# Normalising the two heads of an attention unit together, and copying the compressed probabilities one step earlier, in a two-layer hybrid transformer kernel

## The reference, cut to what matters

```python
o_a = banded_attention(qa, ka, heads(a_v, A_KV_HEADS), A_WINDOW, a_sinks)      # 4 heads, with sinks
o_b = causal_attention(jnp.concatenate([q_nope, q_pe], axis=-1), k_b, v_b)     # 4 heads
o_cmp, o_slc = nsa_compressed_selected(qc, qc_rot, k_cmp, v_cmp, k_slc, ...)   # 8 heads
o_win = banded_attention(qc_rot, k_win, heads(c_vw, C_KV_HEADS), C_WINDOW)     # 8 heads
gates = jax.nn.sigmoid(jax.nn.silu(c_gf) @ c_gate_w + c_gate_b).reshape(b, t, C_HEADS, 3)
o_c = gates[..., 0:1] * o_cmp + gates[..., 1:2] * o_slc + gates[..., 2:3] * o_win
o = jnp.concatenate([o_a.reshape(b, t, -1), o_b.reshape(b, t, -1), o_c.reshape(b, t, -1)], axis=-1)
return o @ w_out
```

## Time and profile before

| what | number |
|---|---|
| time, median of three runs | 1130.08 us (1129.71 to 1130.69) |
| the profiled execution's own time | 1130.08 us |
| its span, first to last instruction | 1128.3 us |
| PE busy | 1084.1 us, 96% of the span |
| DVE busy | 831.3 us, 74% |
| ACT busy | 499.5 us, 44% |
| the chain that ended last | PE 84%, DVE 11%, ACT 2% of the span |
| mean granted clock of PE | 0.989 of full speed |

### The profile page before, as it was taken

How to read it: one execution, slowest core, us unless ns; L and a number is a source line. 1 busy time by engine, 2 the same in 40 slices (tenths; PEclk the granted TensorE clock), 3 DMA queues, 4 the chain that set the end, 5 groups by cost and what they waited for, 6 DMA issues and landing times.

```text
span 1128.3 us, 13797 instructions
## 1 busy us (share of the span) xinstructions
PE 1084.1 (96%) x5221; PEld 837.4 (74%) x5221; DVE 831.3 (74%) x1502; ACT 499.5 (44%) x868; POOL 12.0 (1%) x30
## 2 busy tenths in 40 slices
PE   5999999999989999999999999999998999999998
PEld 1688888865766588888878888886576667888887
DVE  1766997886988785876687789886879787655644
ACT  2543342324567563343534433422255566433431
POOL 4000000000000000000000000000000000000000
PEclk9999999999989999999999999999998999999999
DMA  9799999454612179896439999954582113876631
GB/s 360 259 378 363 372 378 326 148 180 129 224 62 76 38 252 330 305 325 209 162 113 334 342 387 384 355 194 156 115 294 80 53 61 115 269 250 230 199 112 74
DMA packets 149366, 253.70 MB, mean 225 GB/s; under 512 B 9639, under 2 KB 119861, under 8 KB 141109
## 3 DMA queue, kind: packets, MB, share of 16 engines
q1 hardware_dynamic: 148596, 251.53, 65.1%
q10 hardware_dynamic: 704, 1.30, 0.3%
HBM read 251.76 MB, written 1.05 MB: 224 GB/s over the span
## 4 chain that ended last, share of the span: by engine, by line
PE 84%; DVE 11%; ACT 2%; issue 1%; DMA 1%; SPq 0%; DVEq 0%; ACTq 0%
PE ps L693 12%; PE ps L695 12%; PE ps L694 12%; PE ps L723 8%; PE ps L727 8%; PE ps L725 8%; PE ps L845 6%; DVE mwl L1915 2%; PE ps L705 2%; PE ps L674 1%; PE ps L672 1%; PE ps L673 1%; PE ps L901 1%; DMA wide<-in_ada_w_dram 1%; PE ps L890 1%
## 5 line engine op out<-in xcount | busy, mean ns | idle before, releaser
L693 PE MATMUL ps<-wh,uh 128*128 128x512 f32 x576 | 227.2, 395 | 0.0
L695 PE MATMUL ps<-wlo,uh 128*128 128x512 f32 x576 | 224.5, 390 | 0.0
L694 PE MATMUL ps<-wh,ul 128*128 128x512 f32 x576 | 224.3, 389 | 0.0
L1645 DVE TENSOR_TENSOR wlo<-wide,wh 128x1024 fp32r<-128x1024 f32 x176 | 207.6, 1220 | 15.7 <-ACT wh L1183 13.9
L1183 ACT CAST wh<-wide 128x1024 fp32r<-128x1024 f32 x176 | 175.9, 1049 | 16.7 <-DMA wide<-in_ffn_w_in_dram 16.7
L1255 ACT ACTIVATE fs<-ps 128x512 f32<-128x512 f32 x40 | 24.0, 599 | 282.3 <-PE ps L695 273.1
L1800 DVE TENSOR_TENSOR fa<-fs,ps 128x512 f32<-128x512 f32 x40 | 27.5, 688 | 137.8 <-ACT fs L1255 137.2
L723 PE MATMUL ps<-th,fh 128*128 128x512 f32 x320 | 128.1, 400 | 0.0
L695 PEld LDWEIGHTS ps<-wlo,uh 128*128 128x128 f32 x576 | 108.1, 188 | 23.0
L727 PE MATMUL ps<-tlo,fh 128*128 128x512 f32 x320 | 125.0, 390 | 0.0
L725 PE MATMUL ps<-th,fl 128*128 128x512 f32 x320 | 124.6, 390 | 0.0
(11 more groups left out here) (363 smaller groups left out, 1548.2 us busy)
## 6 DMA issues: line engine op xcount, KB each, us to landing
wide<-in_ffn_w_in_dram SPq DMA_DIRECT2D x176, 512.0 KB, 6.6
ada<-in_ada_w_dram SPq DMA_DIRECT2D x60, 1024.0 KB, 7.1
tall<-in_ffn_w_out_dram SPq DMA_DIRECT2D x44, 1024.0 KB, 5.2
wide<-in_w_in_dram SPq DMA_DIRECT2D x14, 1024.0 KB, 7.5
tall<-in_w_out_dram SPq DMA_DIRECT2D x8, 1024.0 KB, 8.6
ada<-in_ada_w_dram SPq DMA_DIRECT2D x16, 512.0 KB, 5.9
wide<-in_c_cmp_w_dram SPq DMA_DIRECT2D x4, 1024.0 KB, 10.1
wide<-in_w_in_dram SPq DMA_DIRECT2D x4, 832.0 KB, 7.9
```

The lines of the kernel that those rows point to most:

```text
L693: mm(o, uh[:, k, rows_], wh[:, hsl, :, k, :], start=(k == 0), stop=False, skip_group_check=True)
L694: mm(o, ul[:, k, rows_], wh[:, hsl, :, k, :], start=False, stop=False, skip_group_check=True)
L695: i = mm(o, uh[:, k, rows_], wlo[:, s, :, k, :], start=False, stop=(k == KD - 1), skip_group_check=True)
L1645: tt(wlo[:, n % 2, :, ks, :], raw, wh[:, (n + 1) % 2, :, ks, :].bitcast(F32), ALU.subtract)\
```

## The change

There are two edits. `normalise` is called once for a unit. It waits for the exponents of both heads, adds the sinks of both in one instruction, takes four reciprocals in one instruction and multiplies by four gates in one; the four scalings stay as they were, head 0 first. And ACT's copy of `cmpT` moves from behind `exponents(4, 0)` to the start of step n = 4.

```diff
                 for n in range(1, NU + 1):
+                    if n == 4:
+                        out_of(l, "cmpt", cmpT[:, :, :])
                     if n == 1:
                         out_of(l, "cq0", cqT[:, 0:2, :])
...
-                        if n == 4 and i == 0:
-                            out_of(l, "cmpt", cmpT[:, :, :])
                         if n >= 3 or i:
                             turned_probs(n - 1, i)
...
-                def normalise(n, i):
-                    br, hh = UNITS[n][0], 2 * UNITS[n][1] + i
-                    st = stat[:, n % 2 * 2 + i, :]
-                    e = E(n, i)
-                    dve.wait_ge(exp_ready, head_at(l, n, i))
+                def normalise(n):
+                    br, pair = UNITS[n]
+                    st = stat[:, n % 2 * 2:n % 2 * 2 + 2, :]
+                    dve.wait_ge(exp_ready, head_at(l, n, 1))
                     if br == "a":
-                        link(tt(st[:, 4:6], st[:, 4:6], st[:, 6:8], ALU.add))
-                    link(V.reciprocal(st[:, 4:6], st[:, 4:6]))
+                        link(tt(st[:, :, 4:6], st[:, :, 4:6], st[:, :, 6:8], ALU.add))
+                    link(V.reciprocal(st[:, :, 4:6], st[:, :, 4:6]))
                     if br in ("slc", "win"):
-                        g = gates[:, :, hh, 1 if br == "slc" else 2]
-                        link(tt(st[:, 4:6], st[:, 4:6], g, ALU.mult))
-                    ts(e[:, 0:P], e[:, 0:P], st[:, 4:5], None, ALU.mult)
-                    ts(e[:, P:3 * P], e[:, P:3 * P], st[:, 5:6], None, ALU.mult).then_inc(en_ready, 1)
+                        g = gates[:, :, 2 * pair:2 * pair + 2, 1 if br == "slc" else 2].rearrange("p t h -> p h t")
+                        link(tt(st[:, :, 4:6], st[:, :, 4:6], g, ALU.mult))
+                    for i in range(2):
+                        e = E(n, i)
+                        ts(e[:, 0:P], e[:, 0:P], st[:, i, 4:5], None, ALU.mult)
+                        ts(e[:, P:3 * P], e[:, P:3 * P], st[:, i, 5:6], None, ALU.mult).then_inc(en_ready, 1)
...
                     if n < NU:
-                        for i in range(2):
-                            normalise(n, i)
+                        normalise(n)
```

## The result

The changed kernel takes **1121.49 us** (median of 4 runs, 1120.81 to 1122.15), beside 1129.89 us of the kernel before in the same comparison: a ratio of 0.9922, 95% interval 0.991 to 0.9934. It is faster by 8.4 us. 1123.0 us and a gain of 7.04 were forecast; the range began at 1122.0, 0.5 us above the median. The four runs lie in two pairs, two at 1120.8 to 1120.9 and two at 1122.1 to 1122.2; the profiled one, 1122.08, is of the upper pair. In the profiled executions the span fell from 1128.3 to 1120.3 us, by 8.0.

What follows compares the result with a forecast made beforehand. PE was taken to bound the kernel, except where it idles for cmpT in each layer's mixer. Gains of 3.51 and 3.53 us, together 7.04, off 1130.08 gave 1123.0 us; range 1122.0 to 1126.8.

Steps and rivals of the forecast that it cites:

- The copy: ACT's cmpT copy would start at 328.81 us, in 1.89 us of idle time, costing ACT nothing; 1.4 us of slack.
- Rival 3: The copy does not come earlier because its transposes come late; nothing won, 1130 to 1131 us; chance 0.07.
- The hole and the clock: First mix_out of each layer: starts 1.72 us earlier and regains 1.79 or 1.81 us of low clock; 3.51 and 3.53.
- Rival 1: The clock still falls at the first mix_out in both layers: 1126.6 us; in one only, about 1124.8; chance 0.12.
- The pairing ahead of the hole: Units 0 to 3: waiting for the second head makes DVE 0.47 us late at unit 3, delaying PE's transposes.
- 0.1 early: DVE after unit 2, if that unit's exponents were in at once: 0.1 us early instead of 0.47 late.
- The price of four numbers: An instruction on four numbers was taken as 0.16 us; at 0.45 the two reciprocals on the path add 0.58 a layer.
- From unit 4 on DVE waits for PE anyway, so the saving there is worth nothing.: Small instructions dropped on DVE in units from 4 on were counted as gaining nothing.
- They move along: Work behind the first mix_out is PE's own chain; PE's progress releases later blocks' transfers, so they shift with it.
- Rival 4: DVE's new waits, 0.66 us in units 6, 8 and 10, reach PE and lose 2 us a layer: 1127; chance 0.04.
- Rival 2: The clock falls earlier, in the thin stretch ahead of 326 us, and stays down; slower, up to 1135 us; chance 0.03.

Runs made afterwards that it cites:

- e6: The changed kernel unaltered, run and profiled a second time; 1122.08 us, ratio 0.9932.
- e5: Kernel before, with the first quarter of the first mix_out computed three more times, discarded, ahead of the wait for cmpT; 1127.66 us.
- e9: The changed kernel with the pairing kept in unit 9 alone, all other units normalised head by head; 1121.26 us.
- e10: The changed kernel with unit 9 alone normalised head by head, all other units paired; 1122.55 us.
- e1: Kernel before with only the copy of cmpT moved, normalise still once for a head; 1122.96 us.
- e8: The changed kernel with the second layer's modulation weight transfers, from the third piece on, cut to half their bytes; 1121.97 us.

## Why the prediction came out as it did

**The copy.** Right in place, cover and price: 327.78 against the 328.81 forecast from the row of before (that execution was 1.01 us later at the mixer's start), done 1.65 us ahead of what it had stood behind. Rival 3 is out.

**The hole and the clock.** Right in mechanism: 3.51 and 3.53 forecast; 3.30 and 3.51 in e6, 3.47 and 4.14 in the changed kernel's first profile. The clock's share, 1.79 taken from two rows of before, measured 1.6 by itself in e5. Rival 1 is out: no 0.50 near 333 us.

**The pairing ahead of the hole.** The 0.47 us by which DVE was to be late measures 0.50 in the first layer of the changed kernel (3.97 of e9 less 3.47) and 0.48 in the second of e6 (3.99 less 3.51). Where unit 2 did not wait, in the second layer of the changed kernel and of e10, the holes gave 4.14, some 0.1 us more than head by head, as the "0.1 early" said. So both of the bounds that stood in the prediction, a wait at unit 2 and none, occur. But the lower end that the forecast gave itself, 1122.2, counts 0.39 us a layer for the second of them, where the prediction's own lines make it 0.57 (0.47 late against 0.1 early) and the forecast of 3.53 against 4.14 makes it 0.61. The low first layers of e6 and e10 (3.30 and 3.18) come from a term that the prediction did not have, the low clock on unit 3's scores. The price of four numbers, 0.16 assumed, is 0.17 to 0.18.

**The step that failed** is the sentence "From unit 4 on DVE waits for PE anyway, so the saving there is worth nothing." It holds for every unit but the ninth: with all units but that one paired (e10) 0.03 and 0.02 us are won on the way to unit 9, as many as with none paired (e1). At unit 9 DVE's 0.39 us reach PE by way of ACT: 0.32 and 0.30 us, together 0.62 that the sum did not have. The chain of waits of before showed the place, a piece of 0.13 us ahead of 366.48, and I had taken for a rule over all later units:

```profile
366.35 0.13 issue
366.48 0.52 PE ps L901 x3
```

With this term the sum is 1122.4 us, inside the range.

What is left, 0.9 us up to the median of 1121.49, no single step explains. A unit 2 without wait in one of the layers is worth 0.6 of it, and the kernel before, at 1129.89 instead of the 1130.08 that the sum began from, 0.2. But it is also less than the 1.3 us by which two profiles of the one program differ in the blocks between (the table, e6). On which side of 1122.0 the median fell was chance: the profiled run, 1122.08, and the median of the second series, 1122.08 as well, lie inside the range.

**Everything behind.** "They move along" held in e6 (0.03 us won) and was wrong by 1.29 us for the execution that was profiled first, 1.1 of them in the wait near 657 us; that PE has no gap where the DMA engines are full was true of the one trace that it was read from. Beside e6 the first execution won 0.5 us more ahead of the mixers, 0.2 more in the first and 0.6 more in the second; that both end at 8.0 is chance.

**Rival 4** did not come: DVE waits 0.62 us at unit 6, and its cover of 3.3 us held, since e10 with units 6 and 8 paired loses nothing on the way to unit 9.

**Rival 2** came in one execution, the profiled one of e8, which has both edits of the changed kernel, but as a mechanism and not with the loss that it named: that span is still 4.7 us shorter than before's. Stretches of 2 us:

```profile
869.00:871.00 2.00, 1.21 (x7) 0.91 (x9) 1.80 (x8) 1.83 (x8) 0.00 (x0) 0.58 0.02 4
871.00:873.00 2.00, 2.00 (x12) 1.24 (x10) 1.97 (x6) 1.12 (x2) 0.00 (x0) 0.50 0.00 0
873.00:875.00 2.00, 2.00 (x12) 1.06 (x11) 1.72 (x11) 1.57 (x5) 0.00 (x0) 0.50 0.00 0
```

The clock is down a second time, in the thin stretch ahead of the first `mix_out` of the second layer, which begins only at 875.60; from 869.79 on the chain of waits lies on PE. The holes of that layer gave 1.19 us, 2.3 less than in e6. The span is 1123.6 us, 3.3 above e6; most of the rest was lost ahead of the first mixer. It belongs to that execution: the median of e8 is 1121.97.

A kernel better than both is suggested, not shown: e9, with the copy and unit 9's pairing alone, has the lowest median and the shortest span (1121.26, 1119.5), but its interval can't be told from the changed kernel's.

## What to carry to other kernels

Here an idle stretch of TensorE of 2.2 us ahead of dense work was paid twice, once as idle time and once as a low clock behind it; filling it with useless work won back the second part, 1.6 us, and moving one copy ahead of a waiting instruction on an in-order engine won both. Where a trace shows a low clock behind an idle stretch, it is worth asking for both parts. When a small instruction is dropped on an engine with slack, follow its result through each later step as far as the bounding engine, since one short wait (here 0.13 us in the chain) shows where the slack is not there. And before explaining a tenth of a per cent from two traces, take a second trace of the same program: here single places differ by up to 1.3 us, and a wait that one trace shows at unit 2 of one layer stands in the other layer of the next.

## What had not been expected of the hardware

The clock does not fall at the same point of the program in each execution. Early in the first mixer the changed kernel stands at 0.50 from 311 to 317 us, and in e6, the same program, it is at 1.00 there and at 0.56 and 0.58 in the stretches from 321 and 323. The wait that comes differs with it: in that layer DVE waited at unit 2 in the one, and for unit 3's scores in the other. Near the program's start before shows 0.50 from 19 to 22 us and the changed kernel 1.00, but e9, which ends earlier than both, is at 0.50 there from 18 to 21: it, too, goes by the execution and not by the change.
